# A two-layer decoder step on one core: an index-key gather, the order of 27 projection units and the order inside the output rounds

## The reference, cut to what matters

```python
q, k, v, qi, ki, wi = split(rmsnorm(h) @ w_attn_in)          # rope on q, k, qi, ki
s      = einsum('bqhd,bsd->bqhs', qi, ki)                    # 4 index heads of width 64
score  = einsum('bqhs,bqh->bqs', relu(s), wi) * IDX_SCALE    # causal
_, idx = top_k(score, 64)                                    # per query
o      = softmax(q . k[idx]) @ v[idx];  h = h + o @ w_attn_out
h      = h + (gelu(conv3(gate)) * val) @ w_ffn_down          # [gate, val] = rmsnorm(h) @ w_ffn_up
h      = h + (gelu(gate) * rglru(conv4(xb))) @ w_rec_out     # [gate, xb] = rmsnorm(h) @ w_rec_in
h      = h + (second MLP);  y = rmsnorm(h)
```

## Time and profile before

| what | us |
|---|---|
| median of three runs | 661.89 |
| the profiled execution, its own time | 664.79 |
| its span, first to last instruction | 663.0 |
| mean granted TensorE clock | 0.959 of full |
| busy: PE, weight load, DVE, ACT, POOL | 605.8, 518.7, 465.8, 365.7, 264.3 |

### The profile page before, as it was taken

One profiled execution on the slowest core, in us unless ns is written; L12 is line 12 of the kernel. 1 busy time (PEld: TensorE's weight loads), 2 busy tenths in 40 slices (PEclk: granted clock), 3 DMA queues, 4 the chain that ended last, 5 costly groups with the idle time before them and its releaser, 6 DMA issues.

```text
span 663.0 us, 12891 instructions
## 1 busy us (share of the span) xinstructions
PE 605.8 (91%) x5102; PEld 518.7 (78%) x5102; DVE 465.8 (70%) x847; ACT 365.7 (55%) x610; POOL 264.3 (40%) x275
## 2 busy tenths in 40 slices
PE   7979576589799999999999999997799999999995
PEld 7857465379687888888888878885588888888884
DVE  4686977744298888878776687786578888785541
ACT  6754444352277666666656559654656666654322
POOL 6661145452033445555200179932244455530002
PEclk9989888888899999999999999999699999999998
DMA  9782459222178767667899864025366666778601
GB/s 258 217 216 76 127 121 339 71 64 64 33 245 276 217 195 200 195 199 222 237 281 260 221 187 132 1 60 163 96 191 194 197 196 198 208 217 244 177 7 66
DMA packets 205574, 113.87 MB, mean 172 GB/s; under 512 B 5649, under 2 KB 202369, under 8 KB 205489
## 3 DMA queue, kind: packets, MB, share of 16 engines
q1 hardware_dynamic: 203097, 106.89, 57.5%
q0 software_dynamic: 2048, 5.79, 2.4%
q10 hardware_dynamic: 368, 0.35, 0.2%
HBM read 109.36 MB, written 3.90 MB: 171 GB/s over the span
## 4 chain that ended last, share of the span: by engine, by line
PE 58%; DVE 15%; issue 14%; ACT 5%; POOL 3%; DMA 3%; SPq 1%; POOLq 1%; ACTq 0%; DVEq 0%
PE acc L1338 17%; PE acc L1340 17%; PE acc L1339 17%; DVE w_lo L876 5%; ACT w_hi L556 3%; POOL area L1702 1%; DVE aL L885 1%; PE misc L1556 1%; DMA stage<-in_w_ffn_up 1%; SPq L435 1%; PE misc L1638 1%; PE acc L1428 1%; PE acc L1429 1%; PE acc L1430 1%; DMA area<-in_cache_kidx,gidx 1%
## 5 line engine op out<-in xcount | busy, mean ns | idle before, releaser
L1338 PE MATMUL acc<-aH,w_hi 128*128 128x264 f16 (+1 forms) x936 | 263.9, 282 | 9.5 <-DVE aL L885 9.2
L1339 PE MATMUL acc<-aL,w_hi 128*128 128x264 f16 (+1 forms) x936 | 263.6, 282 | 0.0
L1340 PE MATMUL acc<-aH,w_lo 128*128 128x264 f16 (+1 forms) x936 | 263.2, 281 | 0.0
L876 DVE SCALAR_TENSOR_TENSOR w_lo<-stage,w_hi 128x1024 f16<-128x1024 f32 (+1 forms) x163 | 215.8, 1327 | 57.7 <-ACT w_hi L556 57.4
L556 ACT ACTIVATE w_hi<-stage 128x1024 f16<-128x1024 f32 (+1 forms) x163 | 180.1, 1106 | 36.2 <-PE acc L1340 27.5
L1338 PE MATMUL acc<-zH,w_hi 128*128 128x264 f16 x424 | 117.1, 276 | 0.0
L1339 PE MATMUL acc<-zL,w_hi 128*128 128x264 f16 x424 | 117.0, 276 | 0.0
L1340 PE MATMUL acc<-zH,w_lo 128*128 128x264 f16 x424 | 117.0, 276 | 0.0
L1338 PEld LDWEIGHTS acc<-aH,w_hi 128*128 128x128 f16 (+1 forms) x936 | 93.6, 100 | 28.0 <-DVE aL L885 11.0
L1339 PEld LDWEIGHTS acc<-aL,w_hi 128*128 128x128 f16 (+1 forms) x936 | 93.6, 100 | 16.2 <-issue 0.3
L1340 PEld LDWEIGHTS acc<-aH,w_lo 128*128 128x128 f16 (+1 forms) x936 | 93.6, 100 | 15.7
(11 more groups left out here) (388 smaller groups left out, 911.9 us busy)
## 6 DMA issues: line engine op xcount, KB each, us to landing
stage<-in_w_ffn_up SPq DMA_DIRECT2D x88, 512.0 KB
...
```

The lines of the kernel that those rows point to most:

```text
L876: v.scalar_tensor_tensor(low, stage[:, place_in_line(u) % 4, 0:n, 0:cols], WSCALE, high, ALU.mult, ALU.subtract).then_inc(lo_done, 1)
L1338: t_.matmul(out, high[:, c, :], xH[:, x0 + c, :], start=first and c == 0, stop=False)
L1339: t_.matmul(out, high[:, c, :], xL[:, x0 + c, :], start=False, stop=False)
L1340: ins = t_.matmul(out, low[:, c, :], xH[:, x0 + c, :], start=False, stop=last and c == n - 1)
```

## The change

It does seven things.

1. The 16 gathers of index keys become one of 128 rows of 4 KB (16 pages of 8 blocks of 16 keys). Two small loads of ACT's queue fetch page number and block number per partition. The keys come out in another layout: PE turns 8 blocks in step 6 and makes 16 products of 128 columns and 8 of one column in step 7 (before: 4 of 257 columns); DVE puts the sample's scores into order by a permuting copy.
2. The index work stands a step or two earlier: prompt scores in steps 4 to 6, sums in step 6, sample scores in 7 and 8, search from step 7 (`take_second` 2, 2, then 2, 1, 1 in steps 7, 8, 13, 14, 15; `take_merged` in steps 9 to 12).
3. `ORDER` has q0 to q5, v0 v1, q6 q7, v2 to v5, k0 to k7, v6 v7: six value units lie in steps 9, 10 and 13 to 16. The key and value gathers are issued in steps 15 to 18.
4. LG becomes 19. The last heads' work of PE stands before chunks 1 to 3 of the output projection, of which four units are made together. Dots j = 0 and 1 stand in step 18, 2 in 19, 3 in 20. `swap_halves` comes before `exp_scores` on ACT. `hi` and `lo` of units 31 to 34 go to homes of their own in steps 28 to 31.
5. In the output rounds `aL` comes ahead of `lo` for chunks 4 to 7 (both k); for k = 1 chunks 0 to 3 have no `hi` and `lo`. The 20 small operations of `softplus` move from step 24 to the first down projection.
6. At the start the sample rows are scaled and turned first, `hi` and `lo` of units 2 and 3 follow all pairs, and the idle products are 4 instead of 22.
7. At the end the scalings of the prompt rows and their stores are in halves, DVE scales the sample rows, and the table of the root is loaded ahead of it.

```diff
-ORDER = ("i0 i1 w0 q0 q1 v0 q2 q3 v1 q4 q5 v2 q6 q7 v3 "
-         "k0 k1 k2 k3 k4 k5 k6 k7 v4 v5 v6 v7").split()
+ORDER = ("i0 i1 w0 q0 q1 q2 q3 q4 q5 v0 v1 q6 q7 v2 v3 v4 v5 "
+         "k0 k1 k2 k3 k4 k5 k6 k7 v6 v7").split()
...
-LG = 17
+LG = 19
+LAST_STEP = LG + 5 + 7
...
+            act.dma_start(ptc[:], a["page_table"].rearrange("s g -> (s g)").unsqueeze(1).to_broadcast([2 * NS, 8]),
+                          allow_slow_non_contiguous=True).then_inc(pages_in, 16)
+            act.dma_start(blkc[:], a["const_a"][0:8, CA_IOTA:CA_IOTA + 1].unsqueeze(0).to_broadcast([2 * NS, 8, 1]),
+                          allow_slow_non_contiguous=True).then_inc(pages_in, 16)
...
+            g.tensor_scalar(gidx[:], ptc[:], 8.0, blkc[:, 0:1], ALU.mult, ALU.add).then_inc(gidx_done, 1)
+            g.indirect_dma_start(out=kx, out_offset=None, in_=a["cache_kidx"].rearrange("a n (b r) d -> (a n b) (r d)", b=8),
+                                 in_offset=bass.IndirectOffsetOnAxis(ap=gidx[:, 0:1], axis=0)).then_inc(kx_in, 16)
...
-            def gather_index_keys(first, n):
...
-                if u == 9:
+                if u == 7:
...
-                    for j in range(4):
-                        ins = t_.matmul(C[0:32, 0:PAST + 1], qz[:, 32 * j:32 * j + 32], kxT[:, j, :], start=j == 0, stop=j == 3)
+                    for odd in range(2):
+                        r = slice(ID * odd, ID * odd + ID)
+                        for s in range(NS):
+                            t_.matmul((C, A)[odd][0:32, 0:P], qz[r, 32 * s:32 * s + 32], kxT[r, :, 16 * s:16 * s + 16],
+                                      start=s == 0, stop=s == NS - 1)
+                    for s in range(NS):
+                        ins = t_.matmul(C[0:32, PAST:PAST + 1], qz[0:ID, 32 * s:32 * s + 32], kiT[0:ID, TP + s:TP + s + 1],
+                                        start=s == 0, stop=s == NS - 1)
...
-                if 8 <= u < 11:
-                    take_second(3 if u == 8 else 2)
-                if 11 <= u < 15:
+                if u in (7, 8):
+                    take_second(2)
+                if u in (13, 14):
+                    take_second(2 if u == 13 else 1)
+                if 9 <= u < 13:
...
+                if u < U_OUT and u not in U_V:
+                    swap_halves(u)
                 if LG + 1 <= u < LG + 1 + H:
                     exp_scores(u - LG - 1)
...
+                if u >= LAST_STEP - 3:
+                    hi(U_OUT + SLOTS + u - (LAST_STEP - 3))
...
-                if 18 <= u < 22:
-                    sample_dots(u - 18)
+                if 18 <= u < 21:
+                    for j in ((0, 1), (2,), (3,))[u - 18]:
+                        sample_dots(j)
...
-                    if k == 1 and 0 < n < DC - 1:
-                        lo(u + 3)
-                    if k == 3 and n < DC - 1:
+                    if k == 3 and n < SLOTS - 1:
                         lo(u + 5)
                     chunk_rest(k, n)
-                if k == 1:
-                    for n in (DC - 2, DC - 1):
-                        lo(r0 + n + 4)
+                    if n >= SLOTS:
+                        lo(u + 4)
...
             def out_ready(c):
-                if c == 0:
-                    pe.wait_ge(o_lo, lows(5) + 1)
-                if c == 5:
-                    turn_token_major(2 * H - 1)
-                    head_out(H - 1)
-                if c >= 6:
-                    pe.wait_ge(o_lo, lows(c))
+                if 1 <= c <= LG + 3 + H - U_OUT:
+                    heads_of_step(U_OUT + c)
+                pe.wait_ge(o_lo, max(lows(c), lows(3) + 1))
...
-            units_together(U_OUT, 3, zH, zL, out_ready)
+            units_together(U_OUT, SLOTS, zH, zL, out_ready)
...
-            pool.wait_ge(fin_r, 1)
-            g.tensor_scalar(ysmp, ysmp, rfin[0:NS, 2:3], None, ALU.mult).then_inc(yt_full[2], 1)
```

232 lines of the change are left out of this document (119 added, 113 removed).

## The result

The changed kernel took 653.07 us (median of four runs, 651.33 to 654.83) against 662.82 us for the kernel before (four runs, 661.49 to 667.14). The ratio is 0.9859, 95% interval 0.9812 to 0.9906, that is 6 to 12 us. The forecast was 638.2 with a range of 628 to 652. The two profiled executions stand 13.2 us of span apart (663.0 and 649.8) and the medians 9.8. So of the miss of 14.9 us, 3.4 are only that single executions of these kernels differ by several us, and 0.9 that the kernel before now has a median of 662.8 and not 661.9. The other 10.5 have their places in the trace.

A forecast was written before the change was run, and what follows sets the result against it. PE fills the MLP stages, so gains lie in attention (DVE's search, then nearly PE) and the output rounds. 10.7 + 11.1 + 0.7 - 4.4 + 0.5 + 3.4 + 1.7 = 23.7 off 661.89 gives 638.2 us, range 628 to 652.

The forecast's parts named there:

- T1: Start to the end of the cast behind DVE's search: cast at 80.2 instead of 90.9 us, gain 10.7.
- T2: From the cast to the last dot: 26.0 us instead of 37.1, gain 11.1.
- T3: Last dot to first output projection chunk: 44.6 us instead of 45.3, a walk of 41.6 plus 3.0 for the clock.
- The rule that speaks against the change: Loops with an idle gap each turn fall to half rate; by it attention's steps 19 to 27 would run at 1.2 GHz.
- rival C: PE's clock falls to 1.2 GHz from step 21 to the last chunk: +30, 668.2 us; chance 4%.
- T4: Units made together in the attention's output projection: four take 14.0 us where three took 9.6, cost 4.4.
- T5: From the end of the four units together to the second MLP: gain 0.5 us.
- softplus at 0: Its 20 small operations, some 3.2 us of DVE, are hidden in the first down projection and cost nothing.
- T6: Recurrent output rounds: period 3.40 us instead of 3.81 and no `lo` in round 3, gain 3.4.
- T7: The end: last scaling of sample rows by DVE instead of POOL, gain 1.7 us, bounds 0 and 2.5.
- Rival A: Heads set attention's pace: logits wait for DVE's maximum, 1.69 us in each of seven steps; time 650.0; chance 20%.
- Rival B: PE still waits for the new gather of index keys in step 6: 9.0 us lost, time 647.2; chance 8%.

The follow-up runs named there:

- Experiment 9: The changed kernel with its one gather of index keys issued in GpSimd's step 5 instead of at the start: 661.41 us, ratio 0.9981 to the kernel before.
- Experiment 12: The changed kernel with three units together instead of four in the attention's output projection: 651.16 us, ratio 0.9757 to the kernel before.
- experiment 8: The kernel before with only the new order of the recurrent output rounds (`aL` ahead of `lo` for chunks 4 to 7): 657.7 us, ratio 0.9951.

## Why the prediction was wrong, step by step

- **T1 was right** (10.7 of 10.7), by errors that cancel: the sums ended at 45.9 and not 45.0; DVE waited for none of the 24 products (3.3 us, not 4.8), where I had 1.7; and it waited 1.03 for a PE product ahead of the cast, which the sum didn't have. Experiment 9 shows the mechanism and its size.
- **T2 failed at "the first lands in time if 0.5 MB moves at the 210 GB/s of rows 1".** I counted each gather as if it had the rate to itself: 2.5 us, where the gathers of keys took 8.1 (median). And I asked whether the gathered keys come in time and not what the gathers keep away. Eight of 0.5 MB, issued in 14 us, stood beside five weight loads and the broadcast queries: some 7 MB, at the 400 GB/s that 88 to 96 us show 17 us. T2 came out 1.5 us over the forecast in the profile that came with the result and 5 to 6 in the others. The trace of before had the same gathers spread over 93 to 113 us. The term's own parts add up to 105.9 and not 106.2, which changes nothing.
- **T3 failed at the clock.** The walk (41.6) was within 0.7 of the length without the clock (42.3). But the row that I cited, 0.84 over 45.4 us, means 14.6 us at the lower level and 7.3 lost in a stretch of 38.0. I put 3.0 where the same share of a longer stretch gives 8, and compared a walk at the full clock with a measured length that had the clock in it. Like for like the work of T3 grew from 38.0 to 42.3. Measured loss: 5.1 to 9.8, 9.4 in this profile. Of the 7.1 missing in T3, 6.4 are this.
- **The rule that speaks against the change came true in part.** The Trainium skill, "TensorE: Matmul & The Clock Gate", section "HAM oscillation", describes a clock that falls again and again in a loop with idle gaps. The trace agrees that it falls again and again, in steps 24 to 27 for 18.9 of 51.7 us, and doesn't for the loop as a whole, nor on the gap: PE was busy without a break from 125.64 to 153, and the clock fell at 147.4. I had made it rival C with one price, +30 for all of it, at 4%. A part of it, 2 to 7 us beyond the allowance, was the likely case, and had no place among my cases.
- **T4 and T5** cost 4.6 where 3.9 was forecast: the four units took 14.8 and not 14.0. Experiment 12 puts 1.3 of it on the fourth unit; the rest, the heads' work between the chunks, was not tested alone.
- **softplus at 0** held in this profile and not in every one: 0 to 1 us of work over all. I named the cover (PE's long chunks) without checking that DVE had the time before the recurrent stage, where PE waits for its last `aL`. The 1.8 us lost in that stretch are a fall of the clock behind PE's wait of 2.90 us, which was 0.82; no term of the forecast had it.
- **T6 was right** (3.6 for 3.4), and experiment 8 shows it alone. **T7** was 1.0 too high, since I let the half stores cost nothing on SP. The 1.4 us of the second MLP stage, for which I had no term, are the clock behind the recurrent rounds: with T6's 3.6 they make the new order worth 5 by the profile.
- Rival A (heads set the pace) didn't come: of the waits for DVE's maximum, priced at 1.69 in each of seven steps, T3 has two, 0.33 and 1.02 us, and with the clock taken out it is within 0.7 of the walk. Rival B's price was right, and its condition wasn't met.
